# Mixer's output projection as seven block products, and the differences of weights formed in the input projection

## What is computed

```python
xn = rmsnorm(x, lw['norm_mix_g'])
... = split_cols(xn @ lw['w_in'], IN_SIZES)          # 3336 columns
# gated DeltaNet, sliding-window attention, short convolution
h = x + jnp.concatenate([out_a, out_b, out_c], axis=-1) @ lw['w_o']
h = h + memory_attend(rmsnorm(h, lw['norm_mem_g']), mem_k, mem_v, lw)
u, ffn_buf_new = causal_dwconv(rmsnorm(h, lw['norm_ffn_g']) @ lw['w_up'], ffn_buf, lw['w_ffn_conv'])
h = h + (jax.nn.silu(ug) * uv) @ lw['w_down']
```

## Time and profile before

| what | us |
|---|---|
| median of 3 runs (lowest to highest) | 1819.88 (1819.06 to 1823.27) |
| the profiled execution | 1819.15 |
| its span in the trace | 1817.8 |
| PE busy | 1751.4 |
| mean granted PE clock | 0.992 of full speed |
| mixer's output projection, first to last product | 629.7 to 731.1 |

### The profile page before, as it was taken

The page is one execution under the profiler, slowest core; times in us unless marked ns, Lnnn a source line. Parts: engine busy times, 40 slices in busy tenths (PEclk is TensorE's granted clock), DMA queues, the critical chain, the costliest instruction groups (busy, mean ns, idle before and its releaser), DMA issues. The chain is left out here.

```text
span 1817.8 us, 27740 instructions
## 1 busy us (share of the span) xinstructions
PE 1751.4 (96%) x10342; PEld 1602.9 (88%) x10342; DVE 1141.0 (63%) x1354; ACT 782.3 (43%) x1489; POOL 767.2 (42%) x644
## 2 busy tenths in 40 slices
PE   6999999999989999999999989999999999999998
PEld 5999999988867788898788879999999999988887
DVE  6325765765666632413536288888888888677874
ACT  5126773325566432312143255444444444443441
POOL 4001212014444272212127428766666666448642
PEclk9999999998989999999999999999999999999999
DMA  6222111224245263124516722222222222397753
GB/s 169 80 56 62 42 36 49 84 85 122 60 135 191 94 234 121 47 105 145 192 68 210 254 67 73 72 72 72 72 72 72 72 72 72 136 377 236 243 190 121
DMA packets 173569, 215.06 MB, mean 118 GB/s; under 512 B 14695, under 2 KB 122600, under 8 KB 171648
## 3 DMA queue, kind: packets, MB, share of 16 engines
q1 hardware_dynamic: 172560, 213.55, 36.0%
q0 software_dynamic: 896, 0.19, 0.1%
q10 hardware_dynamic: 16, 0.00, 0.0%
HBM read 167.11 MB, written 46.60 MB: 118 GB/s over the span
## 5 line engine op out<-in xcount | busy, mean ns | idle before, releaser
L3901 PE MATMUL ffn_banks<-h_parts,up_hi 128*128 128x384 f32 x1920 | 488.7, 335 | 7.6 <-DVE h_parts L4397 4.5
L3901 PEld LDWEIGHTS ffn_banks<-h_parts,up_hi 128*128 128x128 f32 x1920 | 345.7, 188 | 9.7 <-issue 7.8
L3901 PE MATMUL ffn_banks<-h_parts,up_lo 128*128 128x384 f32 x960 | 320.7, 334 | 0.0
L4287 POOL TENSOR_TENSOR up_lo<-up_raw,up_hi 128x512 fp32r<-128x512 f32 x172 | 258.5, 1518 | 105.2 <-ACT up_hi L4056 74.5
L1000 PE MATMUL proj_banks<-x_hi,in_w_hi 128*128 128x384 f32 x624 | 212.6, 341 | 0.5 <-DVE x_lo L251 0.5
L1000 PE MATMUL proj_banks<-x_hi,in_w_lo 128*128 128x384 f32 x624 | 208.7, 334 | 0.0
L1000 PE MATMUL proj_banks<-x_lo,in_w_hi 128*128 128x384 f32 x624 | 208.6, 334 | 0.0
L3901 PEld LDWEIGHTS ffn_banks<-h_parts,up_lo 128*128 128x128 f32 x960 | 180.2, 188 | 0.0
L4337 POOL TENSOR_TENSOR h_parts<-down_cells,h_parts 128x512 fp32r<-128x512 f32 x69 | 103.2, 1499 | 90.4 <-ACT h_parts L4125 90.3
L4012 PE MATMUL ffn_banks<-h_parts,up_hi 128*128 128x512 f32 x352 | 137.1, 390 | 0.0
L4015 PE MATMUL ffn_banks<-h_parts,up_lo 128*128 128x512 f32 x352 | 137.0, 389 | 0.0
(11 more groups left out here) (574 smaller groups left out, 3803.4 us busy)
## 6 DMA issues: line engine op xcount, KB each, us to landing
up_raw<-in_w_up SPq DMA_DIRECT2D x44, 512.0 KB, 3.9
up_raw<-ffn_gated_rows SPq DMA_DIRECT2D x44, 320.0 KB, 5.8
ffn_gated_rows<-h SPq DMA_DIRECT2D x22, 576.0 KB, 2.8
in_w_raw<-in_w_in SPq DMA_DIRECT2D x24, 512.0 KB, 4.0
down_cells<-down_sums SPq DMA_DIRECT2D x44, 256.0 KB, 4.1
up_raw<-ffn_gated_rows SPq DMA_DIRECT2D x33, 256.0 KB, 3.5
down_sums_cells<-in_w_down SPq DMA_DIRECT2D x7, 1024.0 KB, 6.5
down_sums<-down_sums_cells SPq DMA_DIRECT2D x7, 1024.0 KB
```

The costliest lines, as they stand in the source:

```text
L3901: ins = nc.tensor.matmul(banks[:, bank, 0:TC], wt[:, j, k, :], parts[:, q, x, k, :], start=(fresh and n == 1), stop=(n == last), skip_grou ...
L4287: nc.gpsimd.tensor_tensor(w_lo[:, j], weights.full(j), w_hi[:, j].bitcast(F32), ALU.subtract).then_inc(weights.split[j], 1)
```

## The change

The mixer's projection becomes `block_projection`: rows, inner dimension and columns are halved (four row tiles, four slices, 512 columns), and of the eight block products seven remain, on sums and differences of blocks (Winograd's form). The passes come in the order Q1, Q2, Q5, Q6, Q3, Q7, Q4; Q1 and Q2 use plain blocks, the others formed ones. The ninth row tile has no partner and goes as an odd tile with plain blocks in four of the passes (Q1, Q2, Q5, Q3; of Q5 it uses a difference of weights). Differences of activations are formed in place by POOL and DVE (`s1`, `s2`), differences of w_o are read from the scratch. `DownSums` becomes `WeightSums`: 11 steps for w_down and 4 for w_o, all by POOL in the input projection, in four cells that overlay `kv`. POOL forms steps 0 to 2 after pad 1, 3 to 8 after pad 2, 9 to 14 after pad 3. SP loads the first four after the norm, and stores and reloads at tiles 6 to 11. The first silu waits for the stores of cells 0 and 1, the first square for those of cells 2 and 3. ACT and POOL wait at the start of the delta scan until SP has cleared the semaphores of the phase before. The sums leave both output projections. Weights of the mixer's projection come in 28 blocks of 256 KB in place of 8 slices of 512 KB.

```diff
+                    for m in range(C.weight_sums.SLOTS):
+                        C.weight_sums.load(sp, m)
                     for t in range(2):
...
+                for m in C.weight_sums.AT_TILE.get(n, ()):
+                    C.weight_sums.store_and_load(sp, m)
                 if n >= 4:
...
             def silu(m):
                 n, i = convs[m]
                 act.wait_ge(conv_done, m + 1)
+                if m == 0:
+                    C.weight_sums.wait_stored(act, (0, 1))
...
                 act.wait_ge(silu_done, r + 1)
                 if r:
                     act.wait_ge(sq_split, r)
+                else:
+                    C.weight_sums.wait_stored(act, (2, 3))
                 nc.scalar.activation(R.squares, row(r), ACT.Square).then_inc(squared, 1)
...
                                       ).then_inc(padded, 1)
                 if pad >= 2:
                     store_state(pad - 2)
+                for m in C.weight_sums.AFTER_PAD.get(pad, ()):
+                    C.weight_sums.form(pool, m)
...
         def _(act):
+            act.wait_ge(C.semaphores_clear, 1)
...
+class WeightSums:
...
+    SLOTS = 4
+    DOWN = NF // 2
+    STEPS = DOWN + KD // 2
+    AT_TILE = {6: (0, 1), 7: (2, 3, 4), 8: (5, 6, 7), 9: (8, 9), 10: (10, 11, 12), 11: (13, 14)}
+    AFTER_PAD = {1: range(0, 3), 2: range(3, 9), 3: range(9, 15)}
...
+    def load(self, sp, m):
+        if m >= self.SLOTS:
+            sp.wait_ge(self.stored[m % self.SLOTS], 16 * (m // self.SLOTS))
+        sp.dma_start(self.cells[m % self.SLOTS], self.rows[m]).then_inc(self.landed[m % self.SLOTS], 16)
+    def form(self, pool, m):
+        b, done = self.cells[m % self.SLOTS], self.FORMED[m]
+        pool.wait_ge(self.landed[m % self.SLOTS], 16 * (m // self.SLOTS + 1))
+        self.nc.gpsimd.tensor_tensor(b[:, 0, 1], b[:, 0, 1], b[:, 0, 0], ALU.subtract).then_inc(self.formed, 1)
+        pool.wait_ge(self.formed, done + 1)
+        self.nc.gpsimd.tensor_tensor(b[:, 1, 1], b[:, 1, 1], b[:, 0, 1], ALU.subtract).then_inc(self.formed, 1)
+        pool.wait_ge(self.formed, done + 2)
+        if m < self.DOWN:
+            self.nc.gpsimd.tensor_tensor(b[:, :, 0], b[:, 1:2, 1].to_broadcast([P, 2, 512]), b[:, :, 0], ALU.subtract
+                                         ).then_inc(self.formed, 1)
+        else:
+            self.nc.gpsimd.tensor_tensor(b[:, 0, 0], b[:, 1, 1], b[:, 0, 0], ALU.subtract).then_inc(self.formed, 1)
+            self.nc.gpsimd.tensor_tensor(b[:, 1, 0], b[:, 1, 0], b[:, 1, 1], ALU.subtract).then_inc(self.formed, 1)
+    def store_and_load(self, sp, m):
+        sp.wait_ge(self.formed, self.FORMED[m + 1])
+        sp.dma_start(self.kept[m], self.cells[m % self.SLOTS]).then_inc(self.stored[m % self.SLOTS], 16)
+        if self.SLOTS <= m + self.SLOTS - 1 < self.STEPS:
+            self.load(sp, m + self.SLOTS - 1)
+    def wait_stored(self, engine, slots):
+        for i in slots:
+            engine.wait_ge(self.stored[i], 16 * len(range(i, self.STEPS, self.SLOTS)))
+P_Q1, P_Q2, P_Q5, P_Q6, P_Q3, P_Q7, P_Q4 = BLOCK_PASSES = tuple(range(7))
...
+class BlockWeights:
...
+        i = self.place(b)
+        rows = self.raw if i < 6 else self.more
+        return rows[:, i % 6 // 2, 512 * (i % 2):512 * (i % 2) + 512]
...
+    def block(self, b):
+        n, k = divmod(b, self.HK)
+        if n in (P_Q1, P_Q2, P_Q3):
+            row, half = {P_Q1: (k, 0), P_Q2: (self.HK + k, 0), P_Q3: (self.HK + k, 1)}[n]
+            return self.matrix[P * row:P * row + P, 512 * half:512 * half + 512]
+        row, half = {P_Q5: (0, 1), P_Q6: (1, 1), P_Q7: (0, 0), P_Q4: (1, 0)}[n]
+        return self.kept[k, :, row, half, :]
+    def load(self, sp, b):
+        sp.dma_start(self.cell(b), self.block(b)).then_inc(self.landed[self.place(b) // 2], 16)
...
+    near_at, far_at, odd_at = (slice(P * t, P * (t + n)) for t, n in ((near, TILES), (far, TILES), (odd, 1)))
+    L, R = slice(0, 512), slice(512, 1024)
+    s1, s2 = sums_at
+    with C.phase() as ph:
...
+        def takes_of(n, j):
+            if j == TILES:
+                return {P_Q1: ((odd, L),), P_Q2: ((odd, L),), P_Q5: (), P_Q3: ((odd, R),)}[n]
+            return {P_Q1: ((near + j, L),), P_Q5: ((near + j, R), (far + j, R)), P_Q6: ((near + j, R),), P_Q3: ((near + j, R),),
+                    P_Q2: ((near + j, L),), P_Q7: ((far + j, R),), P_Q4: ((far + j, L),)}[n]
...
+        def a_cell(n, k):
+            return {P_Q1: actT[:, k, near_at], P_Q5: s1[:, k, :], P_Q6: s2[:, k, :], P_Q3: s2[:, k, :],
+                    P_Q2: actT[:, HK + k, near_at], P_Q7: s1[:, k, :], P_Q4: actT[:, HK + k, far_at]}[n]
...
+            load_residual((*range(near, near + TILES), odd))
+            load(range(8, 14))
+            load_residual(range(far, far + TILES))
+            load(range(14, 28))
+            sp.wait_ge(stored_too, 32)
+            for n in range(then.weights.RING):
+                then.weights.load(sp, n)
+        @block.tensor
...
+            def fresh(n, j):
+                return n == P_Q1 or (n, j) in Y_TILES
...
+            def one(n, j, k, i):
+                hi, lo = parts_of(n, j, k)
+                a, b = ((hi, b_hi), (lo, b_hi), (hi, b_lo))[i]
+                return nc.tensor.matmul(bank_of(n, j), a, b[:, at(n, k), :], start=(fresh(n, j) and k == 0 and i == 0),
+                                        stop=(k == HK - 1 and i == 2), skip_group_check=True)
+            def turn_early(i):
+                if i == 0:
+                    pe.wait_ge(taken, TAKEN[P_Q3, TILES])
+                if i >= 2:
+                    pe.wait_ge(then.low, i - 1)
+                then.turn_rows(pe, 0, then.ORDER[i], then.early_bank(i))
+            for k in range(HK):
+                for i in range(3):
...
+                        continue
+                    bank_free(n, j)
+                    if j == TILES:
+                        pe.wait_ge(odd_split, 1 if n in (P_Q1, P_Q5) else 2)
+                    for k in range(HK):
+                        if j == 0:
+                            pe.wait_ge(a_split, HK * n + k + 1)
+                            wait_b_split(pe, HK * n + k)
+                        if (n, j, k) in TURN_AT:
+                            turn_early(TURN_AT.index((n, j, k)))
+                        for i in range(3):
+                            ins = one(n, j, k, i)
+                    ins.then_inc(done, 1)
...
+                    act.wait_ge(stored, 16)
...
+            ORDER_OF_SQUARES = tuple(range(NT - 1))
+            for k in range(HK):
+                high_a(P_Q1, k)
+                high_b(P_Q1, k)
+            high_odd(0)
+            for n in BLOCK_PASSES[1:6]:
+                wait_slot(n)
+                for k in range(HK):
+                    high_b(n, k)
+                    high_a(n, k)
+                if n == P_Q2:
+                    high_odd(1)
...
+            for k in range(BY_VECTOR, HK):
+                low_b(P_Q1, k)
+            low_odd(0)
+            for k in range(HK):
+                low_b(P_Q2, k)
+            low_odd(1)
+            for k in range(HK):
+                pool.wait_ge(s1_formed, k + 1)
+                nc.gpsimd.tensor_tensor(s2[:, k, :], s1[:, k, :], actT[:, k, near_at], ALU.subtract).then_inc(s2_formed, 1)
+            for n in (P_Q5, P_Q6):
+                for k in range(HK):
+                    low_b(n, k)
+            for k in range(HK):
+                pool.wait_ge(a_split, HK * P_Q6 + k + 1)
+                nc.gpsimd.tensor_tensor(s2[:, k, :], actT[:, HK + k, near_at], s2[:, k, :], ALU.subtract).then_inc(s3_formed, 1)
+            for k in range(HK):
+                low_b(P_Q3, k)
+            for k in range(HK):
+                pool.wait_ge(a_split, HK * P_Q5 + k + 1)
+                nc.gpsimd.tensor_tensor(s1[:, k, :], actT[:, k, near_at], actT[:, k, far_at], ALU.subtract).then_inc(s1_again, 1)
+            for n in (P_Q7, P_Q4):
+                for k in range(HK):
+                    low_b(n, k)
...
+            def take(n, j):
+                if (n, j) not in DONE:
+                    return
...
...
+            dve.wait_ge(stored_too, 32)
+            for k in range(HK):
+                nc.vector.tensor_tensor(s1[:, k, :], actT[:, k, far_at], actT[:, HK + k, far_at], ALU.add).then_inc(s1_formed, 1)
+            for j in range(TILES + 1):
+                take(P_Q1, j)
+            for n in (P_Q2, P_Q5, P_Q6):
+                for j in range(TILES):
+                    low_a(n + 1, j)
+                    take(n, j)
+                take(n, TILES)
+            for j in range(TILES):
+                take(P_Q3, j)
+                low_a(P_Q7, j)
+            take(P_Q3, TILES)
+            wait_b_split(dve, HK * P_Q3 + 1)
+            then.scale(dve, 0)
+            take(P_Q7, 0)
+            for k in range(HK):
+                low_a(P_Q4, k)
+            take(P_Q7, 1)
+            take(P_Q7, 2)
+            then.early_low(dve, 0, done)
+            take(P_Q7, 3)
```

(60 more changed lines are left out.)

237 lines of the change are left out of this document (179 added, 58 removed).

## The result

The change makes the kernel slower by half a per cent: 1829.2 us (median of 8 executions, 1825.2 to 1833.2) beside 1818.8 for the kernel before (8 executions on the same chip, 1815.3 to 1823.3). The ratio is 1.0053, with a 95% interval from 1.0038 to 1.0068. The prediction was 1820.3 us, with a range from 1810.5 to 1830 and "the same" as the likeliest of the three classes; "slower", which by its own threshold (above 1825.3) is what came, had 0.28.

The account below looks back on a forecast made before the run. The prediction took TensorE (PE), busy 96%, as the bound. Its terms, -9.9 + 9 + 1 + 0.3 = +0.4 us on 1819.15 us, gave 1819.6, or 1820.3 us as median, with a range from 1810.5 to 1830.

Parts of the forecast that it names:

- -9.9: Mixer's projection: 48 fewer products save 10.9 us, less 1 us of stalls; -9.9 us, from -10.9 to -5.9.
- +9: Input projection: waits for late stores and DVE's slowed operations together cost 9 us, bounds 0 and 22 us.
- the clock's +1: Lower PE clock after a stall of this size: 1 us added, from 0 to 3.
- +0.3: Ahead of the delta scan: ACT and POOL wait for cleared semaphores, 0.3 us, from 0 to 1.
- the 1 us of stalls: Mixer's projection: DVE's operations waiting for POOL stall the stage by 1 us, from 0 to 5.
- The rule given for what would prove me wrong: Signs against the forecast: first silu near 149 or 170 us, or PE gaps above 3 us in the mixer's projection.
- +7 to +8 us: Input projection: square waits for stores until 160 us, so PE's low part comes at 164 or 165 us, not 157.36.
- +3 us: Input projection, DVE's side: seven operations with two SBUF operands wait for POOL, delaying the gates PE needs by 3 us.
- each tile's weights are needed two tiles later, which covers it: Input projection: SP is held by the sums' transfers, but weight tiles still arrive in time; no cost.
- 2 to 4 us more: Input projection: by the skill's port rule 12 DVE operations instead of 7 wait for POOL, sum 2 to 4 us higher.
- the stores come late: Rival, input projection: stores at 313 GB/s hold silu and square until some 175 us; +12 us, 1832 us; chance 0.25.
- the case that they cancel: Whole kernel: the mixer's projection gain and the input projection loss cancel, 1815 to 1825 us; chance 0.43.

Follow-up runs that it names:

- the run without sums: Changed kernel without the fifteen steps of sums in the input projection, plain weights read instead: 1814.7 us, ratio 0.9977 to the kernel before.
- the queue alone: Changed kernel with all loads and stores of the sums kept but nothing formed by POOL: 1827.0 us, ratio 1.0048 to the kernel before.
- POOL alone: Changed kernel with POOL running all fifteen steps but no loads or stores of the sums: 1816.4 us, ratio 0.9989 to the kernel before.
- the split: Changed kernel with seven w_down steps back in the memory's output projection, stores earlier, two first loads later: 1814.5 us, ratio 0.9964 to the kernel before.
- the version with both edits: Changed kernel with seven steps moved back, stores and loads re-timed, and DVE's last take before two row scalings: 1812.4 us, ratio 0.9958 to the kernel before.

## Why the prediction was right in its range and wrong in its middle

1829.2 us lies 0.8 us inside the upper end of the range, and four of the eight executions lie above it. That is closer to luck than to foresight: the range reached so far for stores that would be far too late, and a good part of the 10.4 us came from other places. In the sum, -9.9 was -10.3, a term of +3.1 was missing, +9 was +11.3 without its clock, the clock's +1 was +4.9, and +0.3 was 0; the lags of the table that are left, the window stage's 3.65 above all, add 3.4 net, clock included, to make 12.4 in the profiled execution.

**What bounds, and the product count: right.** PE was the bound, 384 products at 0.227 us gave -10.3 us, and DVE didn't starve; the 1 us of stalls was 0.6.

**The end of the mixer's stage: left out, the first step that failed.** The sum "-9.9 us" stopped at the last product. The new order of DVE's queue and ACT's squares behind it added 3.1 us, and behind the wait of 4.8 us PE's clock was low at the start of the query projection, 2.2 us more. So the part was worth -5, and the run without sums measures -4.1. The rule given for what would prove me wrong, gaps above 3 us in the mixer's projection, looked at the inside of the stage and not at its end.

**The input projection: the term "both together make +9 us" was mis-sized; it measured +14.5 us** (14.0 in the trace, of which 2.7 are clock). PE's waits between 139 and 165 us, where it was expected to stand for 8 to 10 us, were 8.5. But it did not stand for the low part of the squares, on which "+7 to +8 us" was worked out; it stood for DVE's gather behind the silu, and so for the store of step 13. By its parts:

- *Queue.* I took 385 GB/s between reads alone (414) and reads with writes (282, 313 at full share), from 74 us on, and got 160 us for the last store. The queue alone went at 368 GB/s and landed it at 160.3. The end was hit, the price of it less well: "+7 to +8 us" became 8.75 us of waiting, with lost clock behind it, 10.1 us in the trace and 12.2 in the medians.
- *POOL.* I had its steps end after 142 us and called the queue the later of the two. In the full change the two wait for each other: POOL idles 13.6 and 4.8 us for loads, then six of its last eleven steps take 6.0 to 8.0 us instead of 5.1 to 5.4, beside DVE, and it ends at 162.7; the queue's rate falls to 346 GB/s. The last store lands at 167.5 instead of 160.3, and the silu goes 4 us later than with the queue alone. This coupling was in no term. Its price was small: 12.2 and 1.7 us, each half alone, leave 0.6 of the 14.5, less than the scatter.
- *DVE's side.* "+3 us" was too high if taken alone: 1.7 us with POOL alone. The operations named for it were the right ones: three taps at 144.5 us took 7.13 us instead of 4.41.
- *Start.* A wait at 64.6 us, 2.0 us and 1.3 of clock, wasn't foreseen: I said of SP that "each tile's weights are needed two tiles later, which covers it", but four loads of 1 MB ahead of that tile made it land at 60.3 us, when it was wanted at 59, and DVE's low part behind it then met POOL and took 3.04 us instead of 1.23. Neither was in a term, and it took both to make the full 2.0.

The Trainium skill (SBUF — State Buffer, section "SBUF: two separate sides") holds that an operation in a two-port mode is locked out like one with two SBUF operands. The trace now agrees, as far as it goes (it tells no modes): beside POOL a copy of 24 columns took 1.28 us where it took 0.17 before, and the single-input first tap 1.87 us instead of 0.82.

```profile
101.35 1.87 DVE L1249 TENSOR_SCALAR room<-room,vec 128x1168 f32<-128x1168 f32 x1
103.25 5.82 DVE L1252 SCALAR_TENSOR_TENSOR room<-room,vec 128x1168 f32<-128x1168 f32 x2
...
142.38 1.28 DVE L1263 COPY room<-room 128x24 f32<-128x24 f32 x1
```

The 2 to 4 us more that were worked out from this didn't arrive: POOL alone costs 1.7 us.

**The clock: +1 us, too small.** Three places behind new or longer waits cost 1.3, 1.4 and 2.2 us, 4.9 in all, above the bound of 3. The 3.3 us in the window stage are not counted here, as they come and go between executions.

**The other terms.** The wait for cleared semaphores (+0.3) was nothing: 1.42 us between last input product and first of the scan, 1.43 before. Everything behind the query projection together gave -0.8 against 0. The delta scan added 0.5, for which there was no term.

**The rivals.** The one that happened is "the stores come late". It was to decide once the last stores end after 164 us; the last ended at 167.5 and the time was 1829.2, near its 1832. Its reason was half right, and so was its price: PE idled 7.3 us at that place, not "about 20". The rate wasn't below the 360 GB/s I named when the queue had only itself to wait for (368), and was below it (346) beside POOL. The Trainium skill (DMA: Bandwidth & Descriptors, Specifications) gives 358 GB/s per core, by which I had the stores at 167 us and 1825 to 1827. The measured rates do not bear it out as a limit here. The middle of the stretch, in the changed kernel, is above it, as is the mean of the queue alone (368):

```profile
105.00:135.00 30.00, 30.00 (x179) 25.74 (x178) 9.74 (x10) 5.11 (x10) 29.20 (x20) 1.00 1.03 398
```

So the skill's figure came out near the right time by a limit that isn't there, which is luck: with a share of 1.03 in this window reads and writes together reach 398 GB/s, and what fell short were the stretches before and after it (236 GB/s from 74 to 90 us, 311 from 150 to 160). With two resources each close to its deadline, and one waiting for the other, the case that they cancel deserved less than 0.43, and the late one more than 0.25.

## What to carry to other kernels

Work moved into a stage with idle engines is free only up to the deadline of its buffers: here 15 steps reused a buffer that was wanted at 149 us, and the traffic alone filled the time up to 160. Eight steps cost next to nothing, and so did all the traffic when it started 10 us earlier and nothing was formed; all fifteen steps, formed and stored earlier, still cost 6 us. Move what is needed early, and leave under its old cover what is needed late. When a stage gets shorter, follow it through to the first product of the next one: what DVE and ACT still owe at its last product does not shrink with it, and behind such a wait (4.8 us here) PE's clock was low in every trace, which is paid once more.

## What the hardware showed that was not expected

Loads and stores of 1 MB, two to four of them queued, kept the DMA engines at 368 GB/s and a share of 0.98 over 86 us; where one of each kind was under way, in 5 us of the memory projection of the kernel before, it had been 282 GB/s at 0.90.

TensorE's clock falls in some executions at waits where it holds in others. The window stage has two waits of about 2 us; the windows behind them, first of the split alone, then of the version with both edits (its waits are 2.2 and 2.0 us, the other's 2.0 and 2.0):

```profile
539.00:544.00 5.00, 5.00 (x29) 3.84 (x28) 4.90 (x8) 2.42 (x4) 4.35 (x6) 1.00 0.54 183
560.00:565.00 5.00, 5.00 (x34) 3.85 (x33) 3.68 (x5) 4.70 (x15) 2.53 (x2) 1.00 0.07 23
```

```profile
540.00:545.00 5.00, 5.00 (x19) 3.66 (x19) 4.90 (x7) 3.00 (x6) 3.69 (x6) 0.66 0.43 146
560.00:565.00 5.00, 4.89 (x18) 3.70 (x20) 3.65 (x7) 5.00 (x15) 3.30 (x2) 0.66 0.34 106
```

The stage, from the last product of the scan to the first of the mixer's projection, was 3.0 us longer in the second. The start of the delta scan does the same. Behind a wait of 2.61 us in both, first the kernel before, then the split:

```profile
407.00:421.00 14.00, 11.48 (x64) 10.26 (x68) 5.71 (x11) 3.40 (x9) 4.79 (x5) 0.51 1.07 311
407.00:421.00 14.00, 11.64 (x179) 10.57 (x180) 6.91 (x13) 4.44 (x10) 7.42 (x9) 0.88 1.08 327
```

The scan took 125.9 us in the first and 122.9 in the second. The changed kernel had the low clock there (0.51), the queue alone the high one (0.88), and the experiments' edits don't touch the scan. So 3 us of the distance between the profiled executions of the kernel before and of the split are not the change's. That explains why two profiles can differ by some us where nothing in the kernels does, and why the difference of two spans is to be read stage by stage.
